# A decoder step on one Trainium2 core: the feed-forward stage in Strassen's form, its weight sums made by accumulating DMAs

## The reference, cut to what matters

```python
def merge_and_ffn(x, ya, yb, yc, oa, gates, gain, wa, wb, wc, wo, g_ffn, w_gu, w_dn):
    ...
    x = x + merged @ wo
    h = rmsnorm(x, g_ffn)
    a, u = jnp.split(h @ w_gu, 2, axis=-1)
    return x + (jax.nn.silu(a) * u) @ w_dn
...
y_prompt = rmsnorm(xp, norm_final)
y_sample = rmsnorm(xs, norm_final)
```

## Time and profile before

| | us |
|---|---|
| median of 3 runs | 992.39 |
| lowest, highest | 991.3, 994.58 |
| the profiled execution, its own time | 996.81 |
| span of its trace | 995.0 |
| TensorE busy | 967.9 (97%) |
| VectorE busy | 507.7 (51%) |
| ScalarE busy | 335.9 (34%) |
| GpSimd busy | 77.6 (8%) |

### The profile page before, as it was taken

The page is one execution under the profiler, slowest core; times in us unless marked ns, Lnnn a source line. Parts: engine busy times, 40 slices in busy tenths (PEclk is TensorE's granted clock), DMA queues, the critical chain, the costliest instruction groups (busy, mean ns, idle before and its releaser), DMA issues.

```text
span 995.0 us, 18231 instructions
## 1 busy us (share of the span) xinstructions
PE 967.9 (97%) x7611; PEld 945.0 (95%) x7611; DVE 507.7 (51%) x933; ACT 335.9 (34%) x559; POOL 77.6 (8%) x107
## 2 busy tenths in 40 slices
PE   6999999999999899999999999999999999999997
PEld 5899999999989889899999999999999999999997
DVE  5735556544887472635355565554445555333232
ACT  7344223444544350422222342222222222222222
POOL 0100013011210200111023000000000000000000
PEclk9899999999999999999999999999999999999999
DMA  7582326432320766122222345222222222222302
GB/s 240 153 262 42 48 77 95 156 108 77 98 65 1 218 192 200 43 86 85 86 86 85 127 147 189 85 88 92 99 96 95 86 85 75 85 75 80 111 1 91
DMA packets 104909, 104.77 MB, mean 105 GB/s; under 512 B 11130, under 2 KB 101752, under 8 KB 104492
## 3 DMA queue, kind: packets, MB, share of 16 engines
q1 hardware_dynamic: 101224, 92.51, 30.3%
q0 software_dynamic: 3552, 11.08, 3.7%
q10 hardware_dynamic: 52, 0.01, 0.0%
HBM read 97.74 MB, written 15.45 MB: 114 GB/s over the span
## 4 chain that ended last, share of the span: by engine, by line
PE 86%; SPq 3%; DVE 3%; ACT 2%; issue 2%; DMA 1%; POOL 1%; ACTq 0%; DVEq 0%; POOLq 0%
PE acc L466 74%; SPq L698 3%; PE acc L1168 1%; PE acc L1081 1%; POOL mt L854 1%; PE acc L1057 1%; PE acc L935 1%; PE acc L924 1%; PE acc L895 1%; PE acc L1041 1%; PE acc L1252 1%; ACT h_hi L1562 1%; DVE w_lo L449 0%; PE acc L1069 0%; DVE mt L1670 0%
## 5 line engine op out<-in xcount | busy, mean ns | idle before, releaser
L466 PE MATMUL acc<-h_hi,w_hi 128*128 128x256 f32 (+1 forms) x1520 | 462.0, 304 | 3.1 <-DVE w_lo L449 2.1
L466 PE MATMUL acc<-h_lo,w_hi 128*128 128x256 f32 (+1 forms) x1520 | 439.2, 289 | 0.0
L466 PE MATMUL acc<-h_hi,w_lo 128*128 128x256 f32 (+1 forms) x1504 | 433.0, 288 | 0.0
L466 PEld LDWEIGHTS acc<-h_hi,w_hi 128*128 128x128 f32 x1520 | 287.6, 189 | 12.0 <-issue 5.1
L466 PEld LDWEIGHTS acc<-h_lo,w_hi 128*128 128x128 f32 x1520 | 288.0, 189 | 4.1 <-issue 2.4
L439 ACT ACTIVATE w_hi<-raw 128x1024 fp32r<-128x1024 f32 (+1 forms) x135 | 140.9, 1043 | 444.9 <-PE acc L466 444.9
L466 PEld LDWEIGHTS acc<-h_hi,w_lo 128*128 128x128 f32 x1504 | 285.0, 189 | 0.0
L449 DVE TENSOR_TENSOR w_lo<-raw,w_hi 128x1024 fp32r<-128x1024 f32 (+1 forms) x134 | 164.0, 1224 | 107.6 <-ACT w_hi L439 102.9
L466 PE MATMUL acc<-s_hi,w_hi 128*128 128x256 f32 (+1 forms) x352 | 101.6, 288 | 0.0
L466 PE MATMUL acc<-s_lo,w_hi 128*128 128x256 f32 (+1 forms) x352 | 101.3, 288 | 0.0
L466 PE MATMUL acc<-s_hi,w_lo 128*128 128x256 f32 (+1 forms) x352 | 100.7, 286 | 0.0
(11 more groups left out here) (348 smaller groups left out, 1122.6 us busy)
## 6 DMA issues: line engine op xcount, KB each, us to landing
raw<-in_w_in SPq DMA_DIRECT2D x25, 1024.0 KB, 5.3
raw<-in_w_gate_up SPq DMA_DIRECT2D x22, 1024.0 KB, 4.9
raw<-in_w_down SPq DMA_DIRECT2D x8, 1024.0 KB, 4.7
rev<-tab POOLq DMA_DIRECT2D x1, 4352.0 KB, 19.4
ring<-in_cache_dsa_kv SPq DMA_DIRECT2D x4, 1024.0 KB, 7.3
raw<-in_w_out SPq DMA_DIRECT2D x4, 1024.0 KB, 5.1
out<-in_cache_dsa_kv SPq DMA_DIRECT2D x2, 2016.0 KB
ring<-in_cache_moba_k SPq DMA_DIRECT2D x48, 64.0 KB, 2.1
```

What stands on the lines that cost most here:

```text
L466: ins = nc.tensor.matmul(acc[:, bank, 0:HALF[half]], a[:, k, :], two(b[:, kx + k, :], half), start=first and k == k0 and c == 0, stop=last ...
```

## The change

**Products.** In the feed-forward stage, two row tiles, two column tiles and two token halves of 272 columns form a 2 x 2 matrix product, which is made with 7 products instead of 8. A `pair` is 256 output columns; there are 38 of them: 22 for gate and up with 4 pairs of row tiles each, and 16 for w_down, whose 22 row tiles are cut in four chunks of 2, 3, 3 and 3 pairs of row tiles (`KPS`). A product of a pair takes 3 x depth matmuls of 272 columns. The order of the products is in `stream`; mostly, for pair n: 1 of n, 4 and 3 of n-1, then 6, 5, 7, 2 of n.

**Weight sums.** Products 5, 6, 3 and 7 need sums of weight tiles. SP loads two quarter blocks once more into `wsum` (L560, `first_terms`), and GpSimd issues four accumulating DMAs for each pair (L1003): one by itself for product 7 (`alone`), and three that follow from each other, for products 5, 6 and 3 (`chain`).

**Splits.** The weight tiles of each product are split by ScalarE (L1769, `w_highs`) and VectorE (`w_lows`) into a ring of six places. The activations get seven forms each (`h7`, `s7`), made by VectorE (`b_sum`), split as before.

**PSUM.** Partial results are shared between products by copying a bank to another (ScalarE, L1790, `bank_seeds`) before the next product adds to it.

**The rest.** `xT` is multiplied by the inverse of `rstd`, so the results of gate, up and down are combined with one operation each; the final norm gets a correction factor (`rtok`). The products of gate, sigmoid and up are made on VectorE, as before, in other pieces. Some semaphores are merged.

```diff
+        def follows(n):
+            return n == 0 or (pairs[n][0] == "down" and pairs[n - 1][0] == "up")
+        stream = []
+        for n in range(NPAIR):
+            if follows(n):
+                if n:
+                    stream += [(n - 1, 4), (n - 1, 3)]
+                stream += [(n, p) for p in (1, 5, 6, 2, 7)]
+            else:
+                stream += [(n, 1), (n - 1, 4), (n - 1, 3)] + [(n, p) for p in (6, 5, 7, 2)]
+        stream += [(NPAIR - 1, 4), (NPAIR - 1, 3)]
+        pos = {np_: i for i, np_ in enumerate(stream)}
+        RING, LEAD = 6, 5
...
+        in_chain = sorted([(tm(pos[n, 1] - 9), n, 5) for n in range(NPAIR)] + [(tm(pos[n, 1] - 6.5), n, 6) for n in range(NPAIR)]
+                          + [(tm(pos[n, 2] - LEAD + 0.4), n, 3) for n in range(NPAIR)])
...
+        def first_terms(sp, n):
...
+            if n >= 2:
+                sp.wait_ge(w_lo_done, n_wout + pos[n - 2, 3] + 1)
...
+                sp.dma_start(w_sum(n, z), src).then_inc(w_loaded[(ffn_load + n) % 3], 16)
...
         def load_weights(sp, n):
             parts, ncol = loads[n]
-            if n >= 3:
+            if n - 3 >= ffn_load:
+                sp.wait_ge(w_lo_done, n_wout + pos[n - 3 - ffn_load, 3] + 1)
+            elif n >= 3:
                 sp.wait_ge(w_lo_done, last_block[n - 3] + 1)
...
+            if n >= ffn_load:
+                first_terms(sp, n - ffn_load)
...
+                    for z, (time, n, p) in enumerate(in_chain):
+                        yield time
+                        if p == 5:
+                            w_ready(pool, n)
+                            if n:
+                                pool.wait_ge(alone, 16 * n)
+                            add_to(w_part(n, 1, 0), w_part(n, 0, 0), alone)
+                        if z:
+                            pool.wait_ge(chain, 16 * z)
+                        if p == 5:
+                            add_to(w_sum(n, 0), w_part(n, 1, 1), chain)
+                        elif p == 6:
+                            add_to(w_sum(n, 1), w_sum(n, 0), chain)
+                        else:
+                            pool.wait_ge(w_lo_done, n_wout + pos[n, 2] + 1)
+                            add_to(w_part(n, 0, 1), w_sum(n, 1), chain)
...
+                def product(i):
...
+                    pe.wait_ge(w_lo_done, n_wout + i + 1)
...
+                    if p in (6, 7):
+                        pe.wait_ge(seeded, seeds[n, "b" if p == 6 else "c"])
+                    if p == 4:
+                        pe.wait_ge(ffn_ev, evacs[n, 7])
...
+                def w_highs():
+                    for i in range(len(stream)):
+                        n, p = stream[i]
+                        yield tm(i - LEAD) + 0.005 if i >= 4 else n_wout - 0.94 + 0.05 * i
+                        w_ready(act, n)
+                        slot_free(act, i)
+                        if p in (5, 6, 3):
+                            act.wait_ge(sem("sum_chain"), 16 * chain_at[n, p])
+                        if p == 7:
+                            act.wait_ge(sem("sum_alone"), 16 * (n + 1))
+                        nc.scalar.activation(w_slot(i, False), w_source(n, p), ACT.Copy).then_inc(w_hi_done, 1)
...
+                        if p == 7 and kind == "gate" and j:
+                            dve.wait_ge(ffn_n2, up_of[j - 1] + 1)
+                        if p in (7, 3):
+                            dve.wait_ge(seeded, seeds[n, "p5" if p == 7 else "u2"])
```

More of the change, by code:

```diff
@@ L187, in build @@
         xT = keep("xT", [P, KD, T])
+        h_at = keep.at
         h_hi = keep("h_hi", [P, KD, T], F32R)
@@ L355, in build, with depth, tm @@
         n_wout = len(blocks)
[L356 to L364, removed]
+        n_all = n_wout
+        ffn_load = len(loads)
+        KPS = (2, 3, 3, 3)
+        FIRST = (0, 2, 5, 8)
+        pairs = []
+        for c in range(len(KPS)):
+            for m_ in range(KPS[c]):
+                pairs.append(("gate", c, FIRST[c] + m_))
+                if m_ == 0 and c > 0:
+                    pairs += [("down", c - 1, j) for j in range(KD // 2)]
+                pairs.append(("up", c, FIRST[c] + m_))
+        pairs += [("down", len(KPS) - 1, j) for j in range(KD // 2)]
+        NPAIR = len(pairs)
+        for kind, c, j in pairs:
+            if kind == "down":
+                k0 = 2 * FIRST[c]
+                loads.append(([(0, 0, rows(w_dn, k0, k0 + 2 * KPS[c], 2 * j * P, 256))], 2 * P))
+            else:
+                loads.append(([(0, 0, rows(w_gu, 0, KD, (D_FF if kind == "up" else 0) + 2 * j * P, 256))], 2 * P))
+        def depth(n):
+            return KPS[pairs[n][1]] if pairs[n][0] == "down" else KD // 2
+        def follows(n):
[11 more added lines that the diff above has]
+        RING, LEAD = 6, 5
+        B_SLOT = {1: 0, 3: 1, 2: 2, 5: 3, 6: 4, 7: 5, 4: 6}
+        def tm(i):
+            return n_wout + 0.25 * i
         w_loaded = [sem(f"w_loaded{i}") for i in range(3)]
@@ new lines, in build @@
+        evacs = {np_: i + 1 for i, np_ in enumerate(urgent)}
+        copies = []
+        for i, (n, p) in enumerate(stream):
+            if p in (1, 5, 6):
+                copies.append((i, n, {1: "b", 5: "p5", 6: "c"}[p]))
+                if p == (5 if pos[n, 6] < pos[n, 5] else 6):
+                    copies.append((i, n, "u2"))
+        seeds = {(n, what): i + 1 for i, (_, n, what) in enumerate(copies)}
+        ffn_ev, seeded, ffn_n2 = sem("ffn_ev"), sem("seeded"), sem("ffn_n2")
+        b_lo, b_hi = sem("h_lo_done"), sem("h_hi_done")
@@ new lines, in second_norm, with claim @@
+                    for i in range(NT + 1):
+                        n = P if i < NT else TS
+                        ins = nc.tensor.matmul(acc[0:n, OLD[4], 300 + i:301 + i], ssq[:, P * i:P * i + n], ones[:, 0:1], start=True, stop=True,
+                                               skip_group_check=True)
+                    ins.then_inc(sem("ssq_mm"), 1)
+                def claim(n):
+                    for name in ("b", "c"):
+                        nc.tensor.matmul(bank(n, name), h7_hi[:, 0, 0, 0:P], h7_hi[:, 0, 0, :], start=True, stop=True)
@@ new lines, in gating @@
+                def gating():
+                    for n, (kind, c, j) in enumerate(pairs):
+                        if kind == "gate":
+                            yield lag(n, T_SIG)
+                            act.wait_ge(ffn_ev, evacs[n, 3])
+                            act.wait_ge(ffn_n2, n + 1)
+                            if j >= 1:
+                                act.wait_ge(sem("t_done"), 2 * j)
+                            else:
+                                act.wait_ge(sem("ssq_done"), KD)
+                            for m in range(2):
+                                nc.scalar.activation(sg[:, m, :], ga[:, m, :], ACT.Sigmoid).then_inc(sem("sg_done"), 1)
+                        if kind == "up":
+                            for part, count in ((slice(0, 4), 16 + 4 * j + 1), (slice(4, 7), 16 + 4 * j + 4)):
+                                yield lag(n, T_BHI + part.start / 4)
+                                act.wait_ge(sem("b_sum"), count)
+                                b_his(4 + j, part, s7_hi[:, j - FIRST[c]])
@@ L1713, in add_squares @@
[L1713 to L1727 removed]
+                            add_squares(k, 0)
```

464 lines of the change are left out of this document (345 added, 119 removed).

## The result

The changed kernel takes **1356.49 us** (median of 4 runs, 1352.51 to 1358.39) beside 992.05 us for the kernel before; the ratio is 1.366, 95% interval [1.362, 1.370]. The forecast was 1070 us, 970 to 1135: slower was right, the size was not, and the time lies outside the range.

What follows compares the result with a forecast made beforehand. TensorE's number of matmuls bound the kernel; 49.7 us of them go, but the loop of waits makes the stage 471 instead of 397.9 us: 996.81 + 73 + 4 = 1074, less 4.4 to the median, so 1070 us, range 970 to 1135.

Steps and rivals of the forecast that it cites:

- The ring: Feed-forward loop: load, issue, three sums, conversion, each waiting for the one before; 13.7 us a gate/up turn, +73 us in all.
- The price of a sum: Each accumulating DMA in the loop lands like GpSimd's nearest store, plus 0.1 us hand-over: 2.7 us for 256 KB.
- Rival C: Sums in the feed-forward stage: adding doubles the data time, 3.6 us for a sum, 1153 us in all; chance 0.11.
- Rival A: Feed-forward loop as short as the smallest rows, 1.96 us a sum, 10.2 us a gate/up turn: 974 us; chance 0.16.
- The load: SP's two quarter blocks for a pair, taken as one DMA of 512 KB: 3.4 us, bounds 2.4 and 4.9.
- issue and conversion: In the loop at depth 4: GpSimd's issue of product 7's sum 0.78 us, conversion by ACT and DVE 1.42 us.
- Rival D: GpSimd's DMA issues in the loop held up by VectorE, half of 142 lengthened by 0.9 us: 1134 us; chance 0.09.
- Rival B: Feed-forward loop doesn't bind, one wait being met earlier than read; only the matmuls count: 947 us; chance 0.07.
- the cost of the form: Added VectorE and ScalarE work in the feed-forward stage stays hidden behind TensorE and costs nothing.
- I cost both at nothing: Both are VectorE's 10.0 of 10.55 us and ACT's under 8 us per gate/up pair; 6 us if cover is gone.
- The end: Behind the feed-forward stage: two last tiles ready together, one more square and scale, added halves, corrected norm: +3 us.

## Why the prediction was right and wrong

**The ring: right.** The five links and their order are those of the timeline, TensorE stands ahead of product 4 as forecast (230 of 314 us of its idle time), and shortening the ring without changing its work shortened the time (1246 and 1148 us).

**The price of a sum: the step that failed.** The term "one sum in the chain", 2.7 us from GpSimd's stores, was 6.8 + 3.6 + 4.3 = 14.7 us a turn instead of 8.1. The neighbours lengthened only the sum for product 5: the sum for product 7 by 1.2 us and the 1024 KB load by 1.0, by the runs without them. The adding lengthened all three: they landed after 6.6, 3.3 and 4.2 us against 5.9, 2.3 and 2.7 for copies, the longer issue included, and the run with copies was 116 us shorter. Of the 4.1 us by which the sum for product 5 exceeds 2.7, about 1 us stays open; it is issued right behind the sum for product 7, and no run has it with neither neighbour. I had priced each sum as if it were alone and a copy. Rival C's 3.6 us met exactly the sum for product 6, the one that runs alone; it was meant as the far end. Its second reason, the 1024 KB load beside the sums, was real at the sum for product 5 only. Rival A is out: the quickest of the 152 sums of the changed kernel landed after 2.7 us. The range was drawn from spreads of 0.35 us a sum, where the miss was 2.2 us in the mean.

**The load:** 4.11 us against 3.4, with upper bound 4.9; **issue and conversion** 0.75 and 1.38 us against 0.78 and 1.42. So of the 7.2 us by which a turn of depth 4 exceeds 13.7, the sums are 6.6 and the load 0.7. Over the 35 turns the excess is 704 - 450 = 254 us of the 286 that were missed, some 16 of them in the two turns with a cache copy. The rest is before the first of them and behind the last, where the forecast had 471 - 450 = 21 us and the trace has 12.4 (583 to 595.4) and 36.7 (1299.3 to 1336); there the sums also stand in line.

**Rival D: wrong mechanism.** Issues were 0.88 to 1.8 us, as it asked for, but with copies in the place of sums and the same VectorE work they are 0.55 and 0.75: what makes them long is the adding, not VectorE.

**Rival B and the cost of the form: wrong.** "I cost both at nothing" was tested by the run without sums: 1004.5 us against B's 947. VectorE's busy time, forecast as 10.0 of 10.55 us in a pair of gate and up, wasn't the limit: in that run it is 9.1, as in this stretch of one gate and one up pair (columns as in rows 3).

```profile
803.72:825.89 22.17, 21.30 (x169) 21.10 (x169) 18.19 (x32) 13.70 (x27) 0.00 (x0) 1.00 0.42 131
```

What the busy time didn't show were the hand-overs: a product that waits for a PSUM copy by ScalarE (17.5 us in all, one 2.7 us gap after another at the end), then the clock that falls after the gaps. The 49.7 us of saved matmuls were spent on these. The share of the clock in the 21 us of longer matmuls, some 15, is an estimate; no run separates it.

**The end: right, by a small term.** From the last product to the end of the span 17.9 us (1332.8 to 1350.7) against 13.7 (981.3 to 995.0): +4.2 where +3 was forecast (the fourth of the +4 stood at the entry, and no run separates it there).

The Trainium skill's fit for a DMA of GpSimd ("DMA: Bandwidth & Descriptors", Anatomy of one DMA) gives 2.6 us as an estimate for 256 KB. The copies agree where they are alone (2.3 and 2.7); for the accumulating DMAs the measurement decides, 3.3 to 6.6.

## What to carry to other kernels

Before a fixed chain of DMAs is put behind a stage that is bound by TensorE, write down one turn of it, price each link beside what runs with it at that moment, and compare it with the time of one unit of TensorE's work; a lead of several units hides a delay, not a period. Give each result that others wait for its own semaphore: three sums that counted on one cost some 200 us here together with their order (a semaphore of its own for the last sum in another order, 5, 6, 3, gained nothing: 1379 us). And ask what the saving is worth when the new step is free, before its price is worked out: here nothing.

## What the runs showed of the hardware

- An accumulating DMA of 256 KB within SBUF lands in 3.3 to 4.2 us with no other sum beside it and in 5.9 to 6.6 beside another one and a 1024 KB load; a plain copy in 2.3 to 2.7 and 5.9 to 6.0. Its issue holds GpSimd 0.88 to 1.8 us, a copy's 0.55 to 0.75.
- With sums of 16 KB the sum for product 5 still took 4.3 us in the median where that for product 6 took 2.35: so a transfer that moves little is lengthened too when a load of 1024 KB is in flight and another sum was issued just ahead; which of the two does it was not separated.
- Behind a cache copy of 2016 KB the sum for product 5 took 15.5 and 13.3 us, where others of the same sizes took about 6.9 and 3.9.
- VectorE's low part of 128 x 512 took 1088 ns instead of 687 while GpSimd made additions in SBUF.
- The granted clock, 1.00 in the whole stage before, was 0.77 in the mean with gaps of some 10 us in each pair, and 0.82 at the end of the run without sums, where gaps of 2.6 us stood between products.
